# High and low weights side by side: the layout of TensorE's weights, word by word in one tile

## What is computed

```python
# first block
z = rmsnorm(x) @ w_in + b_in
y = concat(silu(layernorm(conv31(z_a * sigmoid(z_gate)))), pooled(z_p))
h = x + y @ w_out
h = h + (silu(n @ w_gate) * (n @ w_up)) @ w_down        # n = rmsnorm(h), width 2816
x = rmsnorm(h)
# second block, two layers: attention, then a feed-forward network with a 3-tap convolution
for layer in range(2):
    x = layernorm(ALPHA * x + attention(x) @ w_attn_out)
    x = layernorm(ALPHA * x + (silu(g) * val) @ ffn_w_out)   # g, val = conv3(x @ ffn_w_in)
```

## Time and profile before

| | us |
|---|---|
| median of 3 runs | 1811.39 |
| the runs | 1809.56 to 1812.52 |
| profiled execution, its own time | 1808.84 |
| span of that execution | 1807.0 |
| PE busy in it | 1762.7 |
| POOL busy | 1032.3 |
| ACT busy | 796.0 |
| DVE busy | 765.9 |

### The profile page before, as it was taken

The page is one execution under the profiler, slowest core; times in us unless marked ns, Lnnn a source line. Parts: engine busy times, 40 slices in busy tenths (PEclk is TensorE's granted clock), DMA queues, the critical chain, the costliest instruction groups (busy, mean ns, idle before and its releaser), DMA issues.

```text
span 1807.0 us, 26859 instructions
## 1 busy us (share of the span) xinstructions
PE 1762.7 (98%) x8755; PEld 1476.5 (82%) x8755; DVE 765.9 (42%) x1382; ACT 796.0 (44%) x1674; POOL 1032.3 (57%) x926
## 2 busy tenths in 40 slices
PE   8999999999999999999999999999999999999997
PEld 6879888888887888788888888877777888888887
DVE  7973000001235556553333322487875533333224
ACT  5644332322245555464444422555565644444231
POOL 6966555555562333466666665655554666666651
PEclk9999999999999999999999999999999999999999
DMA  4312333333334454223333233333332233332332
GB/s 153 94 47 82 105 93 93 93 88 109 94 89 115 126 134 120 85 75 100 103 94 93 82 110 88 82 93 78 86 82 71 72 110 97 93 101 82 105 91 98
DMA packets 327252, 171.94 MB, mean 95 GB/s; under 512 B 43458, under 2 KB 316948, under 8 KB 327188
## 3 DMA queue, kind: packets, MB, share of 16 engines
q1 hardware_dynamic: 327172, 171.12, 33.7%
q10 hardware_dynamic: 16, 0.00, 0.0%
HBM read 152.15 MB, written 2.10 MB: 85 GB/s over the span
## 4 chain that ended last, share of the span: by engine, by line
PE 86%; DVE 9%; ACT 2%; issue 1%; POOL 1%; DMA 0%; DVEq 0%; SPq 0%; ACTq 0%
PE bank L983 24%; PE bank L985 23%; PE bank L984 23%; DVE score L2266 3%; PE attended L983 2%; PE attended L984 2%; PE attended L985 2%; PE turned L1424 1%; PE attended L1440 1%; PE bank L1056 1%; PE bank L1068 1%; DVE xres L2165 1%; PE bank L1069 0%; PE score L1417 0%; PE score L1407 0%
## 5 line engine op out<-in xcount | busy, mean ns | idle before, releaser
L742 POOL TENSOR_TENSOR WL<-raw,WH 128x512 fp32r<-128x512 f32 (+3 forms) x656 | 777.6, 1207 | 539.8 <-ACT WH L1605 537.2
L983 PE MATMUL bank<-XL,WH 128*128 128x512 f32 x1432 | 568.5, 397 | 3.7 <-DVE work L2577 1.2
L985 PE MATMUL bank<-XH,WL 128*128 128x512 f32 x1432 | 557.9, 390 | 0.0
L984 PE MATMUL bank<-XH,WH 128*128 128x512 f32 x1432 | 557.3, 389 | 0.0
L1605 ACT ACTIVATE WH<-raw 128x512 fp32r<-128x512 f32 (+3 forms) x656 | 338.4, 566 | 293.2 <-PE bank L985 186.5
L985 PEld LDWEIGHTS bank<-XH,WL 128*128 128x128 f32 x1432 | 269.4, 188 | 56.9
L983 PEld LDWEIGHTS bank<-XL,WH 128*128 128x128 f32 x1432 | 269.7, 188 | 55.9 <-DVE work L2577 1.5
L984 PEld LDWEIGHTS bank<-XH,WH 128*128 128x128 f32 x1432 | 269.9, 188 | 50.3
L983 PE MATMUL bank<-HL,WH 128*128 128x512 f32 (+1 forms) x528 | 198.6, 376 | 0.0
L985 PE MATMUL bank<-HH,WL 128*128 128x512 f32 (+1 forms) x528 | 198.4, 376 | 0.0
L984 PE MATMUL bank<-HH,WH 128*128 128x512 f32 (+1 forms) x528 | 198.4, 376 | 0.0
(11 more groups left out here) (366 smaller groups left out, 2524.9 us busy)
## 6 DMA issues: line engine op xcount, KB each, us to landing
raw<-in_ffn_w_in SPq DMA_DIRECT2D x88, 512.0 KB, 3.7
raw<-in_w_gate SPq DMA_DIRECT2D x22, 512.0 KB, 3.6
raw<-in_w_up SPq DMA_DIRECT2D x22, 512.0 KB, 3.7
raw<-in_ffn_w_out SPq DMA_DIRECT2D x28, 384.0 KB, 3.2
raw<-in_ffn_w_out SPq DMA_DIRECT2D x28, 320.0 KB, 3.2
raw<-in_a_w_in SPq DMA_DIRECT2D x16, 512.0 KB, 3.9
raw<-in_kv_w SPq DMA_DIRECT2D x32, 256.0 KB, 3.0
raw<-in_w_in SPq DMA_DIRECT2D x12, 512.0 KB, 3.7
```

What stands on the lines that cost most here:

```text
L742: pool.tensor_tensor(wl, x, wh, ALU.subtract).then_inc(w_lo, 1)
L983: pe.matmul(out_, wh, xl, start=start, stop=False)
L984: pe.matmul(out_, wh, xh, start=False, stop=False)
L985: return pe.matmul(out_, wl, xh, start=False, stop=stop)
```

## The change

WH and WL become the two halves of one tile, `weights`, in which the last index chooses high or low: a high word, its low word, the next high word, and so on. A block of 128 high weights is now every second word of 1024 bytes, and the block of the low weights the words between them. All that uses WH and WL (`high`, `low`, `step`, `half_item`, `stage_in_halves`, `first_items` and others) is unchanged: it reaches them through the two views.

A new tile `odd_line` of 16 words, which nothing uses, stands ahead of `weights`, so that this begins at byte 74048, which is 64 past a multiple of 256. The five tiles behind it (`par`, `ones`, `identr`, `masks`, `work`) and `small` also move by 64 bytes. `small` gets 16 words smaller, so that everything from `HH` and `xin` on lies where it lay. XH, XL, HH, HL, OH, OL begin at multiples of 256 as before. No instruction is added, removed or moved on any engine; the number of words that each reads and writes is the same, and only steps and addresses differ.

```diff
@@ -220,15 +220,16 @@
         yout = sb("yout", [P, 2 * QT, S])
         last_rows = sb("last_rows", [P, DT, S])
         raw = sb("raw", [P, RAW, DT, P])
-        WH = sb("WH", [P, SLOTS, DT, P], F32R)
-        WL = sb("WL", [P, SLOTS, DT, P], F32R)
+        odd_line = sb("odd_line", [P, 16])
+        weights = sb("weights", [P, SLOTS, DT, P, 2], F32R)
+        WH, WL = weights[:, :, :, :, 0], weights[:, :, :, :, 1]
         par = sb("par", [P, 6 * P])
         ones = sb("ones", [P, P])
         identr = sb("identr", [P, P], F32R)
         ident = identr.bitcast(F32)
         masks = sb("masks", [P, 2, P], F32R)
         work = sb("work", [P, 6, S])
-        small = sb("small", [P, 108 + 20])
+        small = sb("small", [P, 108 + 4])
```

## The result

The changed kernel takes 1836.88 us, the median of four runs from 1831.38 to 1842.40; the kernel before took 1810.47 beside it (four runs, 1809.52 to 1812.52). The ratio is 1.0144, with a 95% interval of 1.0108 to 1.0181. Forecast were 1745 us and a range of 1733 to 1818. So the loss is 19 to 26 us, and its size scatters more between executions than the time of before does.

A forecast was written before the change was run, and what follows sets the result against it. PE's 7055 matmuls, by the spacing of their starts, were taken as the bound: 7055 x 11.0 ns = 77.6 us, 86% kept is 66.7, other edits nothing, so 1811.4 - 66.7 = 1744.7 us; range 1733 to 1818.

The forecast's parts named there:

- a floor near 216: Lowest spacing of 512-column matmul starts: 213.3 ns of streaming plus 2.3 for the change of weights, 215.6 ns.
- the 10 ns: Part of the 13.3 ns added to each matmul's streaming time that is not the change of weights, at 512 and 256 columns.
- the argument on equal speeds: With every second word, load and stream both move 8 bytes in 0.83 ns, keep their distance, and meet always or never.
- the rows against: Trace rows against meetings: 16-column loads still had 231 ns spacing; a matmul without a load beside it lasted as long.
- The sum: Saving of 11.0 ns on each of 7055 matmuls, 77.6 us, of which 66.7 us reach the end.
- the factor 0.86: PE's share of the chain, 86%, taken as the part of the 77.6 us saving that reaches the end.
- The other edits: Steps in ACT's copies and POOL's work, and tiles moved by 64 bytes: taken as nothing on the path.
- 1: Rival: the 10 ns are the stream's own or an instruction price only shifting with phase; 1811 us within 3; chance 0.23.
- 2: Rival: part of the 10 ns goes, spacing 220 to 224 ns, saving 16 to 41 us; 1770 to 1795; chance 0.17.
- 3: Rival: stepped weight loads take 213 instead of 107 ns, slowing 876 256-column matmuls, 84 us; 1895 or 1840; chance 0.09.
- 4: Rival: POOL's step makes its subtraction line L742 twice as long, bounding gate and up, 86 us lost; 1897; chance 0.04.
- 5: Rival: meetings of load and stream become permanent, 13.3 ns more on each of 7055 matmuls, 81 us; 1892; chance 0.07.

The follow-up runs named there:

- m3: Kernel of matmuls alone on constant operands: stream step varied, with normal or step-0 loads, and weights begun at every 16 bytes; 215.8 to 461.7 ns at 512 columns.
- m2: Kernel of matmuls alone: weights or stream read with step zero, loads of 4 columns, 64 combinations of places; at 512 columns none of these 64 below 226.7 ns.
- m1: Kernel of matmuls alone: contiguous or every-second-word weights, and streams, begun at various places, and shorter loads; 226.7 to 235.6 ns for weights at 512 columns.
- e3: Against the kernel before: ACT and POOL use every second word of one tile, PE reads contiguous blocks of it (result not the reference's); 1811.42 us, ratio 1.0009.
- e2: Against the kernel before: still two contiguous tiles, but WH, WL and the five tiles behind begin 64 bytes past a multiple of 256; 1839.66 us, ratio 1.0163.
- e6: Against the kernel before: weights, streams and all other tiles moved together to 64 bytes past a multiple of 256; 1809.11 us, ratio 0.9994.
- e1: Against the changed kernel: `odd_line` left out, so the interleaved tile begins at a multiple of 256 bytes; 1854.20 us, ratio 1.0248 to the kernel before.
- e5: Against the kernel before: still two contiguous tiles, but WH, WL and the five tiles behind begin 16 bytes past a multiple of 256; 1833.05 us, ratio 1.0125.

## Why the prediction was wrong

**What bounds the kernel** held: PE is busy 98% of either span, and what the distance of starts does, the time does. The distances of before (226.7, 120.0), 0.417 ns a column and a floor near 216 held as well; m3 measured 216.7 with a stream that stands still and 215.8 with one that reads each word twice.

**The step that failed** is "if the 10 ns come from the two reads meeting", with the full saving taken for it. The prediction made one cause out of what was left over between 226.7 and the floor, because it was equal for 256 and 512 columns and looked as if it happened during the next load. m2 and m3 show that this is two cases. At 512 columns, over four fifths of the 7055 matmuls, it goes away only when the stream reads more slowly, and not with the load's reading; at 256 columns 6.7 ns do go away with the load's. And the argument on equal speeds, that load and stream would then never meet and lose nothing, has no place at which it holds: every second word gave 230.0 to 235.6 ns at all sixteen places at 512 columns, and about 120 to 121 at the four places tried at 256, where there was something to win.

**The evidence that was given too little weight** was in the rows against. The earlier trace rows showed loads an eighth as long with 231 ns, which m1 repeats (230.7), and was written down as "more and not less" without a change of the chances. The distances of 0.22 and 0.24 in the earlier trace rows were read as a sign that something can be saved. They mean that the matmuls have several patterns. In the projections before is in the best one found at 512 columns: of over 200 layouts none was below 226.7. In the attentions its own dense distances into `bank` average 230 to 231 ns. From an uneven spacing one could as well have concluded that a change of place may lose.

**The sum** multiplied 7055 by -11.0 ns. Measured are +2.7 ns on some 5800 512-column distances, 15.7 us, the other +1.7 us of the 512-column total in longer distances, and 4.3 us at 256 columns, of which the dense ones have only 0.5 ns x 1131 = 0.6. Together that is 16.3 us from the dense distances, and the profiled span grew by 22.6, 3.5 of it through the clock. So what the dense distances lost arrived in full, and the factor 0.86 was too careful, at least for a loss.

**The other edits** were right. POOL's line was to stay within 5% and has 1%; PE's waits for it were to stay below 5 us and are 1.4; the load was to stay at 188 and has 195, far from 250. ACT was given 0 to 16 ns a copy and takes 40, on an engine with time to spare; e3 shows that all of it costs nothing.

**The rivals.** 1 named the cause rightly for 512 columns, that the 10 ns are the stream's own, but not the result, because its "only shifts with phase" was taken to be free. 2 did not happen. 3 did not: a load with a step takes 7 ns more, not twice as long, and e2 loses at 512 columns without any step. (Its count of 876 matmuls of 256 columns is also short: with the output stages it is 1164, and its price would have been 111 us.) 4 did not (e3). 5 had the right sign and the right place in the sum, matmuls of 512 columns that each cost more, but not the size (13.3 ns forecast, 2.7 measured) nor the shape: at 256 columns the dense distance rose by 0.5. What was missing is a rival "the change of place moves the matmuls into another pattern, better or worse", whose price no row of before could give, but whose sign was open.

**The two rules.** The rule of the Trainium skill that stream and weights have two independent ports ("TensorE: Matmul & The Clock Gate", "Step-by-step: what each phase is for") would have kept the time at 1811. The traces do not bear out that a load takes nothing from the matmul beside it: the place of the weights alone moves the distance from 226.7 to 233.3 ns (e2) and back when the stream moves along (e6), and at 256 columns a load that stays on one word takes it from 120.0 to 113.3 (m2). The rule of the Trainium skill on 16-byte lines ("SBUF — State Buffer", "Specifications (TRN2)"), that two hits in a line suffice for full bandwidth, nearly holds for the load here (195 against 188 ns). It does not for the fp32r stream, which takes 453.3 ns instead of 226.7 with a step of two words (m3).

**What stays open.** What in SBUF makes the unit of 6.67 ns and the 10 ns of a stream at full pace; why the load's movement counts at 256 columns and not at 512; and why the changed kernel scatters from 1827 to 1842 us over the two measurements when before stays within 1807 to 1815. The clock is not the reason for that: 1827.13, 1830.09 and 1839.96 us all had a mean granted clock of 0.995. That the kernel falls into its two patterns, 230.0 and 233.3, in different shares would do it, and e1 has such a change between layers, but for the changed kernel it is argued only: both profiled executions are at 230.

## What to carry to other kernels

What is left between a measured spacing and a computed floor is not yet a cost of the mechanism one has in mind: stop one of the two parties (a step of 0, a load of 4 columns) and see whether it goes, before a sum is built on it. If a tuned layout has an even spacing, and other places of the same kernel an uneven one, moving an operand can lose as well as gain. In a kernel bound by fp32r matmuls of 512 columns keep weights and streams at the same place modulo 256 bytes, and never give the streamed operand a step. A step in the weights is not cheap either: the load itself takes only 7 ns more, but at none of sixteen places did the distance stay at 226.7, and at the same place as before it costs 44 us (e1). A step in what ACT and POOL write cost nothing here, since both had time to spare (e3). And look at the granted clock before explaining the last few microseconds between two executions.

## What the runs showed of the hardware

- A stream of 512 fp32r columns takes 216.7 ns if it reads one word over and over, 215.8 if it reads each word twice, 226.7 at best if it reads a new word each beat, 453.3 with a step of two words and about 460 with four (m3).
- A weight load that stays on one word does not lower the 226.7 ns at 512 columns (229 to 231, m2 and m3), but lowers 120.0 to 113.3 at 256 (m2).
- The place of weights to stream modulo 256 bytes moves the spacing between 226.7 and 235.6 ns at 512 columns, and between 113.3 and some 121 at 256, and the best places differ: 0 for the one, 64 bytes for the other. Moving both together changes nothing (e6).
- The matmuls settle into patterns that repeat over a few of them, whose means are often multiples of 6.67 ns over the pattern. One layout can have two of them and hold each for a whole stage (e1: 235.6 and 233.3; e5: 226.7 and 233.3).
- A load of 128 columns with a step of two words takes 194 to 197 ns in the lines of `product` instead of 188, and up to 202 at the start of a stage; POOL's subtraction with steps takes 1% more, ACT's copy to every second word 6% more.
